# Three passes from split weights for the values, gates and output of the last phase

## What is computed

```python
def hybrid_layer(x, w_in, w_out, ln_g, ln_b, rel_bias, topk):
    proj = jnp.einsum('bsd,dn->bsn', x, w_in)
    qA, kA, vA, gA, qB, kB, vB, gB, qI, kI, wI = jnp.split(proj, SPLIT_POINTS, axis=-1)
    ...
    oA = stick_breaking_attention(heads(qA, HEADS_A), heads(kA, HEADS_A), heads(vA, HEADS_A))
    oB = dsa_sparse_attention(...)
    mix = jnp.concatenate([oA * jax.nn.silu(gA), oB * jax.nn.silu(gB)], axis=-1)
    y = jnp.einsum('bsm,md->bsd', mix, w_out)
    return layer_norm(ALPHA * x + y, ln_g, ln_b)
```

## Time and profile before

| | us |
|---|---|
| median of 3 runs | 2975.58 |
| lowest, highest | 2974.86, 2983.72 |
| the profiled execution's own time | 2977.58 |
| its span in the trace | 2975.8 |
| last phase in the trace | about 2655.5 to 2971.7 |
| of it layer 0, layer 1: first transposes of x to last write of x | 2663.4 to 2818.7, 2817.4 to 2969.0 |

### The profile page before, as it was taken

The page is one execution under the profiler, slowest core; times in us unless marked ns, Lnnn a source line. Parts: engine busy times, 40 slices in busy tenths (PEclk is TensorE's granted clock), DMA queues, the critical chain, the costliest instruction groups (busy, mean ns, idle before and its releaser), DMA issues. The chain is left out here.

```text
span 2975.8 us, 30375 instructions
## 1 busy us (share of the span) xinstructions
PE 2398.3 (81%) x9779; PEld 1605.8 (54%) x9779; DVE 1751.3 (59%) x3656; ACT 908.0 (31%) x1740; POOL 987.2 (33%) x691
## 2 busy tenths in 40 slices
PE   6997999869878898898786986797566467559897
PEld 4776878758663343343333664575345336337575
DVE  3444311032136988988975688587759869755151
ACT  4444222233322222222222443243133324323232
POOL 2332555343232343344342234234323523310001
PEclk9998999989998999999898997899678678759898
DMA  4321333223139899999999899899799999964553
GB/s 158 97 67 50 98 98 101 81 81 126 49 121 347 314 406 415 416 409 402 395 410 405 333 379 372 314 371 394 295 355 384 416 409 398 380 260 172 216 190 140
DMA packets 257323, 805.56 MB, mean 271 GB/s; under 512 B 18366, under 2 KB 139862, under 8 KB 191655
## 3 DMA queue, kind: packets, MB, share of 16 engines
q0 software_dynamic: 73728, 536.90, 44.8%
q1 hardware_dynamic: 183463, 267.06, 25.6%
HBM read 795.07 MB, written 14.07 MB: 272 GB/s over the span
## 5 line engine op out<-in xcount | busy, mean ns | idle before, releaser
L1337 POOL DMA_INDIRECT gathered<-in_peer_rows,experts x436 | 532.5, 1221 | 918.2 <-DVE x_res L2635 607.0
L1695 PE MATMUL peer_banks<-gathered,peer_diags 128*128 128x512 f32 x720 | 338.3, 626 | 56.2 <-ACT peer_diags L1750 56.2
L78 PE MATMUL group_banks<-group_x_t,group_ring 128*128 128x128 f32 (+1 forms) x2016 | 338.1, 331 | 16.7 <-ACT group_x_t L2447 8.4
L2621 DVE CUSTOM_DVE_ANT_0 gathered<-gathered,late_nat 128x1024 f32<-128x1024 f32 x256 | 317.8, 1244 | 35.0 <-DMA gathered<-in_peer_rows,experts 29.9
L2635 DVE SCALAR_TENSOR_TENSOR x_res<-gathered,group_weights,x_res 128x1024 f32<-128x1024 f32 x256 | 331.4, 1295 | 2.7 <-DVE group_weights L2627 0.3
L78 PEld LDWEIGHTS group_banks<-group_x_t,group_ring 128*128 128x128 f32 x2016 | 305.4, 207 | 46.3 <-ACT group_x_t L2447 10.8
L1695 PEld LDWEIGHTS peer_banks<-gathered,peer_diags 128*128 128x128 f32 x720 | 142.2, 201 | 241.7 <-issue 241.7
L2261 PE MATMUL group_banks<-group_ring,group_x_t 128*128 128x512 f32 x512 | 233.7, 611 | 28.4 <-DMA group_ring<-in_weights 28.4
L1790 DVE CUSTOM_DVE_ANT_0 peer_product<-gathered,early_nat 128x1024 f32<-128x1024 f32 x180 | 214.7, 1222 | 37.9 <-DMA gathered<-in_peer_rows,experts 36.6
L1695 PE MATMUL peer_banks<-early_gathered,peer_diags 128*128 128x512 f32 x304 | 149.3, 643 | 51.7 <-ACT peer_diags L1750 51.7
L2261 PEld LDWEIGHTS group_banks<-group_ring,group_x_t 128*128 128x128 f32 x512 | 98.3, 197 | 150.2 <-issue 117.0
(11 more groups left out here) (376 smaller groups left out, 4201.6 us busy)
## 6 DMA issues: line engine op xcount, KB each, us to landing
group_ring<-in_weights SPq DMA_DIRECT2D x270, 512.0 KB, 4.7
mixer_wq<-in_w_in SPq DMA_DIRECT2D x24, 512.0 KB, 4.1
mixer_wk<-in_w_in SPq DMA_DIRECT2D x24, 512.0 KB, 4.1
peer_w<-in_w_pq SPq DMA_DIRECT2D x8, 1024.0 KB
gathered<-in_peer_rows,experts POOLq DMA_INDIRECT x436
diff_wv<-in_w_in SPq DMA_DIRECT2D x8, 512.0 KB, 4.0
conv_wb<-in_w_in SPq DMA_DIRECT2D x8, 512.0 KB, 4.0
merge_w<-in_w_conv_out SPq DMA_DIRECT2D x8, 512.0 KB
```

The source lines that it names most:

```text
L78: last = nc.tensor.matmul(out, lhsT, rhs, start=n == 0, stop=n == len(pairs) - 1)
L1337: nc.gpsimd.indirect_dma_start(row_buffer(m, r), None, A["peer_rows"], bass.IndirectOffsetOnAxis(ap=at, axis=0))\
L1695: last = nc.tensor.matmul(ps[:, ACC[unit % 2] + half, :], diags[:, r % DIAGS, :], row_buffer(m, r)[:, D + half * BANK:D + (half + 1) * BAN ...
L2621: nc.vector.tensor_tensor_reduce(out=row, in0=row, in1=m.late_nat[:, t % 2, :], scale=1.0, scalar=0.0, op0=ALU.mult, op1=ALU.add, accum_ou ...
```

## The change

In the last phase (`parted`), the four `natural` products of a layer and `output` are done in three passes of fp32r parts. For each of the 24 blocks of a layer that these use (`NATURAL`), ACT makes a high part (`high_blocks`) and POOL a low part (`low_blocks`), into 8 slots `parts`. ACT and DVE split the turned input (`high_input`, `low_input`), and `copy_mix` with `low_mix` the turned mix. A slot of the ring is free once its low part is made; the ring has 8 slots. The 12 products over q and k stay as they were. On PE, `output` is cut in two: chunks 0 to 2 stand ahead of `turn_mix(SPARSE)`, chunks 3 to 7 behind it. POOL's list becomes the low parts of the blocks with the four `add_keep` of a layer between them. The phase owns 7 semaphores more.

```diff
@@ -1853,6 +1853,7 @@
 
 WEIGHTS = weight_order()
 BLOCKS = len(WEIGHTS)
+NATURAL = [name for name in WEIGHTS if name[0] == "out" or name[0] in (STICK, SPARSE) and name[1] in "vg"]
...
-    WS = 6
+    parted = not keeps
+    WS, PS = (8, 8) if parted else (6, 0)
...
         ring = sb("ring", [P, WS, D])
+        if parted:
+            parts = sb("parts", [P, PS, 2, D], PART)
+            x_parts, mix_parts = sb("x_parts", [P, 2, KC, NQ], PART), sb("mix_parts", [P, 2, KC, NQ], PART)
+            block_high, block_low = sem("block_high"), sem("block_low")
...
                         l, b = divmod(n - WS, BLOCKS)
                         name = WEIGHTS[b]
-                        if name[0] == "kI":
+                        if parted and name in NATURAL:
+                            sp.wait_ge(block_low, part_at(l, *name) + 1)
+                        elif name[0] == "kI":
                             sp.wait_ge(proj_done, job_at[l, "kI"] + 1)
...
+                def low_blocks(l, kind, name, some):
+                    for b in some:
+                        k = part_at(l, "out", b) if kind is None else part_at(l, kind, name, b)
+                        n = block_at(l, "out", b) if kind is None else block_at(l, kind, name, b)
+                        pool.wait_ge(block_high, k + 1)
+                        low_part(nc.gpsimd, parts[:, k % PS, LOW, :], ring[:, n % WS, :], parts[:, k % PS, HIGH, :]).then_inc(block_low, 1)
...
+                if parted:
+                    for l in range(LAYERS):
+                        low_blocks(l, STICK, "v", range(4))
+                        low_blocks(l, STICK, "g", range(4))
+                        low_blocks(l, SPARSE, "v", range(4))
+                        add_keep(l, 0)
+                        low_blocks(l, SPARSE, "g", range(4))
+                        add_keep(l, 1)
+                        low_blocks(l, None, "out", range(2))
+                        add_keep(l, 2)
+                        low_blocks(l, None, "out", range(2, 4))
+                        add_keep(l, 3)
+                        low_blocks(l, None, "out", range(4, KC))
...
+                def natural_in_parts(l, name, half):
+                    bank = start((l, f"{name}{half}", last))
+                    pe.wait_ge(x_low, l + 1)
+                    for b in range(4):
+                        k = part_at(l, half, name, b)
...
+                        for c in range(2):
+                            passes = three_passes(lambda part: x_parts[:, part, 2 * b + c, :], lambda part: parts[:, k % PS, part, c * HALF:(c + 1) * HALF])
+                            for i, (lhsT, rhs) in enumerate(passes):
+                                made = nc.tensor.matmul(bank, lhsT, rhs, start=b + c + i == 0, stop=b == 3 and c == 1 and i == 2)
...
+                def output_in_parts(l, chunks):
+                    for c in chunks:
+                        if c % 4 == 0:
+                            pe.wait_ge(mix_low, 2 * l + c // 4 + 1)
+                        k = part_at(l, "out", c)
+                        pe.wait_ge(block_low, k + 1)
...
+                    if parted:
+                        output_in_parts(l, range(3))
                     turn_mix(l, SPARSE)
-                    output(l)
+                    if parted:
+                        output_in_parts(l, range(3, KC))
+                    else:
+                        output(l)
...
+                def high_blocks(l, kind, name, some):
+                    if not parted or l == LAYERS:
+                        return
+                    for b in some:
+                        k = part_at(l, "out", b) if kind is None else part_at(l, kind, name, b)
+                        n = block_at(l, "out", b) if kind is None else block_at(l, kind, name, b)
+                        act.wait_ge(w_loaded[n % WS], 16 * (n // WS + 1))
+                        if k >= PS:
+                            act.wait_ge(*part_used(k - PS))
+                        nc.scalar.activation(parts[:, k % PS, HIGH, :], ring[:, n % WS, :], ACT.Copy).then_inc(block_high, 1)
...
+                def high_input(l):
+                    act.wait_ge(proj_copied, job_at[("x", last, 1) if l == 0 else (l - 1, "x", last, 1)] + 1)
+                    nc.scalar.activation(x_parts[:, HIGH, :, :], x_t[:, :, :], ACT.Copy).then_inc(x_high, 1)
...
                 def copy_mix(l, half):
                     for t in tiles:
                         bank = finished((l, f"mix{half}", t))
-                        nc.scalar.activation(mix_t[:, half * 4:(half + 1) * 4, local(t)], bank.rearrange("p (c q) -> p c q", q=P), ACT.Copy)\
+                        into = mix_parts[:, HIGH, half * 4:(half + 1) * 4, :] if parted else mix_t[:, half * 4:(half + 1) * 4, local(t)]
+                        nc.scalar.activation(into, bank.rearrange("p (c q) -> p c q", q=P), ACT.Copy)\
...
                 inverse_roots(0)
+                high_blocks(0, STICK, "v", range(2))
...
                             copy_input(l, t, n)
+                    if parted:
+                        high_input(l)
+                    high_blocks(l, STICK, "v", range(2, 3))
...
                     copy_index_keys(l)
+                    high_blocks(l, STICK, "v", range(3, 4))
                     for n in range(2):
                         done = gelus((l, "qI", n), done)
                         copy_index_queries(l, n)
+                    high_blocks(l, STICK, "g", range(2))
                     done = copy_values(l, STICK, done)
...
+                    high_blocks(l, STICK, "g", range(2, 3))
                     copy_pair(l, 0)
+                    high_blocks(l, STICK, "g", range(3, 4))
...
                             softplus(l, u + 1)
                         else:
                             done = copy_values(l, SPARSE, done)
+                        if u in (1, 2):
+                            high_blocks(l, SPARSE, "v", range(2 * u - 2, 2 * u))
+                        elif u == 3:
+                            high_blocks(l, SPARSE, "g", range(2))
...
                             copy_pair(l, u + 1)
+                            high_blocks(l, SPARSE, "g", range(2, 4))
                             copy_turned(l, u)
...
                         done = gelus((l, "sparse", p, 3), done)
+                        high_blocks(l, None, "out", range(2 * p, 2 * p + 2))
                     copy_mix(l, SPARSE)
                     done = gelus((l, "out"), done)
+                    high_blocks(l + 1, STICK, "v", range(2))
...
+                def low_input(l):
+                    dve.wait_ge(x_high, l + 1)
+                    low_part(nc.vector, x_parts[:, LOW, :, :], x_t[:, :, :], x_parts[:, HIGH, :, :]).then_inc(x_low, 1)
...
+                def low_mix(l, half):
+                    job, four = job_at[l, f"mix{half}", last], slice(half * 4, (half + 1) * 4)
+                    dve.wait_ge(proj_copied, job + 1)
+                    low_part(nc.vector, mix_parts[:, LOW, four, :], ps[:, job % 2, :].rearrange("p (c q) -> p c q", q=P), mix_parts[:, HIGH, four, :])\
+                        .then_inc(mix_low, 1)
...
+                    if parted:
+                        low_input(l)
...
                             apply_gates(l, SPARSE)
+                            if parted:
+                                low_mix(l, STICK)
...
                     gated_sparse(l)
+                    if parted:
+                        low_mix(l, SPARSE)
```

31 lines of the change are left out of this document (29 added, 2 removed).

## The result

The changed kernel takes 3011.91 us (median of 6, 3004.26 to 3019.82), before took 2979.65 beside it: 1.0100 of before, 95% interval 1.0078 to 1.0123, so 30 us slower. A second set gave 1.0108 (1.0086 to 1.0129). Forecast were 21 us more, 2996.8, in a range from 2979 to 3006; 4 of the 15 us between 2996.8 and 3011.91 are the median of before, 2975.58 of the three runs at hand then and 2979.65 of six. The profiled execution took 3007.87 with a span of 3006.1, 30.3 longer than the 2975.8 of before.

The account below looks back on a forecast made before the run. The last phase is one thread through ACT's softplus, DVE's sums and PE's products. Layers +5.4 each (10.8), -1.2 for layer 0, +11.1 start, +0.5 tail: +21.2 us, 2996.8 from 2975.58, range 2979 to 3006.

Parts of the forecast that it names:

- the clock in the waits: `tails` behind the long waits in steps u = 1 and 2 runs at the lower clock: +3.0 us a layer.
- POOL's queue: Sparse steps, g1's end to `sparse_out(7)`: low parts queue with `add_keep` on POOL, +3.0 us, less 1.2 in layer 0.
- the start: Phase start, once: ACT's first copy of x stands behind two high parts waiting for their loads, +11.1 us.
- the hold: Steps u = 1 and 2: DVE's suffix sums wait for POOL's low parts, +4.1 us a time, +8.2 a layer.
- the output: End of `sparse_out(7)` to the end of output: three passes and the cut, -4.8 us a layer.
- the first of the products, v0: v0's product saves 1.4 us on PE, given back on ACT and DVE behind it: 0, between -1.4 and +2.
- ACT waits for weights in the middle too: Rival: g0's high parts wait for blocks in ACT's list, or the search is held: +8 us, 3005, chance 0.09.
- the second: Sign: in steps 1 and 2 suffix sums 2 to 2.7 us, `tails` waiting 4 to 5, first pieces about 2.
- the third: Sign: the four products take 5.4 to 5.6 us.
- half a hold: Rival: DVE's suffix sums meet one low part, not two; wait 2.0 us, +7.0 in all, 2982.6, chance 0.15.
- no hold: Rival: the suffix sums run beside POOL unheld; -4.0 us in all, 2971.6, chance 0.08.
- the start costs nothing: Rival: the loads at the phase's start land in time after all, 2985.7 us, chance 0.08.

Follow-up runs that it names:

- The halves: The changed kernel with each low part on POOL made in two operations of 512 columns instead of one of 1024: 1.0030 of before.
- my own repair: The changed kernel with ACT copying x and layer 0's index keys before making v0's four high parts in layer 0: 1.0074 of before.

## Why the prediction was wrong

Direction and the large mechanisms were right; two costs were left out or taken too small. In the pair of profiles the phase grew by 27.6 where the forecast without its tail has 20.7. The stretch from the index keys to logits 0 is 5.6 of that, the clock in the waits 2.6, POOL's queue 1.4, v1 and g1 0.6; the start, the hold and the output came out 0.5, 0.9 and 1.8 lower than forecast. The later arrival, 2.6, and the 4 us by which the median of before had been drawn low are no part of the sum.

- **The step that failed** is the first of the products, v0, "I count 1.4 given back: 0 (between -1.4 and +2)". Behind v0 the stretch to logits 0 grew by 5.4 and 4.2, while v0's passes gave 1.3 and 2.2 (of the 2.2, 0.6 was a wait for a load inside before's v0). From the index keys to logits 0, both layers together, the four profiles of before have 62.1 to 62.5 and the two of the changed kernel 68.1 and 69.4: +5.6 to +7.3 for 0. With g0 in float32 the sum is 59.0, so g0's parts cost it 9 to 10 and v0's three passes give 3. I had written down all its parts (the loads that free late, ACT's list, the held sum), but treated a chain of waits as cover. The rival "ACT waits for weights in the middle too" named this place and priced it at +8.
- **The clock in the waits**: 1.5 a time, four times, was mis-sized. `tails` 2 to v1 grew by 7.0 and 9.3, less the 3.9 of one wait 3.1 and 5.4: 8.6 instead of 6.0. In layer 1 nearly the whole `tails` ran at the lower clock, not its first pieces alone.
- **The clock at layer 1's start**: no term of the forecast. The +3.8 and -4.2 of the table's second row are where the clock happened to rise in the pair; taken with v0 and what follows they are within the stretch above.
- **The hold**: 4.1 each forecast, 3.9 measured four times (15.5 for 16.4). The halves show a wait by the operation: 2.33 and 2.40 became 1.25 and 1.33. With this the trace agrees with what the Trainium skill says ("SBUF — State Buffer", section SBUF: two separate sides): an exclusive lock, held for the whole instruction.
- **The start**: +11.1 forecast, +10.6 measured. **g0** -1.4, right. **v1 and g1** together -2.6 a layer forecast, -2.3 measured.
- **The output**: -4.8 forecast, -5.8 and -5.6 measured. The cut has less to do with it than the passes.
- **POOL's queue**: +3.0 for layer 1 measured +3.7, +1.8 for layer 0 measured +2.5. `sparse_out(7)` follows a turn at the low clock.
- **The tail**: +0.5 forecast; from the output's end to the last instruction 13.4 became 13.5.

Of the forecast's five signs four showed (in the second, one of the four `tails` began with a piece of 1.31 and not of about 2); the third was off by a little (products of 5.70 to 6.11, not 5.4 to 5.6). The rivals "half a hold", "no hold" and "the start costs nothing" are refuted by the rows above.

## What to carry to other kernels

An engine that is a third busy still has a list: before you put an operation there that waits for a load, ask what stands behind it and who waits for that. This cost 10.6 at the start, 4.8 in my own repair, 10 in layer 1 of the version with the float32 output. Helper work on POOL must be placed where DVE has no operation on the thread that it holds (here those with two inputs in SBUF, and one TENSOR_SCALAR), or be cut into short ones; and it must buy more than it costs. Of the five products here the three that did so were v1, g1 and the output, and that is shown for them together (0.9970); the output alone gave 0.9995. And a stretch that got shorter ahead of a load may have bought nothing: cut behind the wait, not ahead of it.

## What the runs showed of the hardware

- A DVE sum with two inputs in SBUF waits for the POOL operation in progress and for no more: sums of 0.42 took 2.33 beside operations of 1024 columns and 1.25 beside 512, with more POOL work queued behind the first sum in both cases. One TENSOR_SCALAR was held as well (2.46 for 0.49). MAX8 and MATCH_REPLACE8 beside a low part kept their 0.69 and 0.68.
- A `tails` behind a wait of 4.07 ran 4.7 to 6.0 instead of 3.1 to 3.2 (the pieces at the low clock 2.07 and 1.06); behind 1.91 and 1.92, three of four took 4.7 to 4.9 and one 3.2.
- At the start of layer 1 the same PE instructions took 12.4 to 12.9 in the four profiles of before, behind an idle 5.30, and 15.3 to 16.7 in twelve of fourteen with the output in parts, behind 5.30 (once 6.23). In before most of the difference went again in a wait of 0.6 to 2.5 for v0's last block and the lower clock behind it.
